# First stage of a two-block transformer kernel: the residual stream ahead of the gate tiles, one gate tile out of the chunk loop

## The chip, the cores and the metric

The kernel runs on one core of one Trainium2 chip, as one launch. The metric is the device time of that launch in microseconds, the median of several runs. PE is TensorE (its weight loads are shown apart as PEld), DVE VectorE, ACT ScalarE, POOL GpSimd, SP the engine whose queue issues nearly all transfers here.

## The reference, cut to what matters

Two blocks of two layers each work on 512 latent tokens and 256 context tokens of width 1024. The change touches only the very start, the first half of the first layer's mixer:

```python
mod  = silu(c)     @ ada_w[0] + ada_b[0]      # 6 vectors of 1024 for the latent tokens
modc = silu(c_ctx) @ ada_w[0] + ada_b[0]      # the same for the context tokens
sh1, sc1, ... = split(mod, 6)
a  = rmsnorm(h,  norm1_g[0]) * (1 + sc1)  + sh1     # modulate
ac = rmsnorm(hc, norm1_g[0]) * (1 + csc1) + csh1
# even_mixer
u, v, q, k, vv = split(a @ w_in, ...)         # u and v are 512 wide each
...
# chunk_mlp, the gating part of the mixer
u  = gelu(u)
vf = gelu(v);  vf = (vf - mean) * rsqrt(var + eps)   # by groups of 128 columns
mixed = einsum('gpq,bnqgc->bnpgc', w_s, vf) + b_s    # over 128 tokens
out = u * mixed
```

The matrices are drawn in float32. A product of the gate is computed as three products of rounded parts: high by high, high by low and low by high.

## The kernel before, in words

The 768 tokens lie along the free dimension and the 1024 features in 8 chunks of 128 partitions: `k.h` is [128, 8, 768]. The program is a row of stages, each a block with one instruction list for each engine. The first stage, `gating_mlp`, does the following.

**Stream.** `k.h` is loaded, ACT squares each chunk (`StreamSums.scalar`, L582), PE sums the squares over the partitions with a matrix of ones (L565). DVE forms the mean (L809), ACT the root (`norm.roots`, L732), DVE the reciprocal (L813) and its split in a high and a low part (L621, L623), and PE spreads it over all partitions (`norm.tensor`, L631 and L632) into PSUM banks 0 and 1.

**Modulation.** `FirstModulation` needs 16 tiles of 512 KB of `ada_w`, two for each chunk c (shift and scale). `mod.load(sp, c)` issues them (L2201), into places that are free this early: the buffers `mo`, `q`, `key` and `v` and the ring slots 2 to 4. `mod.multiply(pe, c)` makes 32 matmuls (L250), `mod.copy(act, c)` copies the two rows out of PSUM (L2224), `mod.turn(pe, c)` turns them into columns (L2231), and DVE's `mod.finish` adds the bias and makes the gain (L2238, L2241).

**Chunks.** For each chunk DVE scales the stream (`norm.scale`, L781), ACT adds the shift and rounds to the high part (`norm.high`, L748), and DVE makes the low part (`norm.low`, L767). DVE's order is finish(c), scale(c), low(c-1).

**Gate tiles.** The columns of `w_in` come as tiles of 128 columns, [128, 8 x 128], through the ring (`feed.issue`, L141). Each is split in a high part by ACT (`split.write_high`, L204) and a low part by POOL or DVE (`split.write_low`, L211). Entries 0, 1, 2 and 7 are the four tiles of u, entries 3 to 6 those of v. Entry 0 accumulates in PSUM banks 4 and 5, entry 1 in banks 6 and 7, entry 2 in banks 2 and 3, which the modulation uses until its last chunk. `tile_step(n, c)` multiplies chunk c of entry n (L2302, L2303, L2306), and waits for the high and the low part of that chunk. `tile_products` multiplies all chunks of an entry (L228).

**PE's order** is the loop over `step`: multiply(step), tile_step(0, step - 2), turn(step), tile_step(1, step - 4), with the spread behind multiply(0). Steps 8 to 11 do what is left of the two tiles. Then come entry 2 whole, the six token tiles of v, entry 7, and the mixing over tokens.

**SP's queue** is a list written by hand: small vectors, entries 0 and 1, the pick matrix (L262), the stream in four transfers of two chunks, the 16 modulation tiles, and after the third multiply the entries 2 to 7.

Of the kernel before, what the change touches and what calls it, by code (L numbers as in the profile page):

```python
# [16 lines left out]
ACT = mybir.ActivationFunctionType  # L17
AX = mybir.AxisListType

P = 128  # L20
D = 1024
KC = D // P
LAT, CTX = 512, 256
TOK = LAT + CTX
# [300 lines left out]
def spans(tokens):  # L325

    return [(0, LAT, 0), (LAT, TOK, 1)] if tokens == TOK else [(0, LAT, 0)]
# [6 lines left out]
def program(nc, io, out):  # L334
# [4 lines left out]
    with ExitStack() as ctx:  # L339
# [29 lines left out]
        with mixer(k, True, TOK, (4, TOK, 4, 512)):  # L369
            with ExitStack() as k.tmp:  # L370
                gating_mlp(k)
            project_in(k, "diff_in", DIFF_WORK, 5, TOK, rope=True)
# [156 lines left out]
def region(k, r, n=TOK):  # L529

    return k.psf[:, 1024 * r:1024 * r + n]
# [432 lines left out]
def tile_products(k, pe, i, j, dst, src, tokens, split=None, chunks=range(KC), first=True, last=True, between=None):  # L964

    slot = split.wait(pe, i, j) if split else k.feed.wait(pe, i, j)
    for a, b, _ in spans(tokens):
        if a and between:
            between()
        for n, c in enumerate(chunks):  # L970
            lo, hi = first and n == 0, last and n == len(chunks) - 1
            cols = slice(n * P, (n + 1) * P)
            if split:
                mm = split.products_of(pe, dst[:, a:b], (split.high[:, slot, cols], split.low[:, slot, cols]),
                                       (src[0][:, c, a:b], src[1][:, c, a:b]), lo, hi)
            else:
                mm = pe.matmul(dst[:, a:b], k.ring[:, slot, cols], src[:, c, a:b], start=lo, stop=hi)
    if split:
        mm.then_inc(split.products, 1)
    else:  # L980
        k.feed.done(mm, j)
# [1263 lines left out]
def gating_mlp(k):  # L2245

    nc, feed = k.nc, k.feed
    T, G = TOK // P, 4
    with Stage(k, "gating") as st:
        split = Split(k, st, 5, places=(0, 1, 4, 2, 3, 0, 1, 4))  # L2250
        mod = FirstModulation(k, st)
        norm = rms_stream(k, st, TOK, "mixer", 0, bank=3, r=0, squares=k.mo[:, 0:4, :])
        norm.by_pool, norm.shifts = (), k.mod[:, 0:KC, :]
        h_landed = [st.sem(f"h_landed{n}") for n in range(4)]
        ones_ready, loaded = st.sem("ones_ready"), st.sem("stream_loaded")
        sums = StreamSums(k, st, TOK, 3, loaded, 0, [norm.sq[:, c, :] for c in range(4)])
        u, v = k.q, k.v
# [9 lines left out]
        ENTRY = (0, 1, 2, 7)  # L2267
        U_REGION, MIX_REGION, V_BANK = (2, 3, 1, 3), (0, 1, 0, 1), (0, 1, 4, 5)

        @st.block.sync  # L2270
        def _(sp):
            sp.dma_start(k.small[:, :], k.io["small"]).then_inc(mod.small_landed, 16)
            for e in range(2):
                feed.issue(sp, 0, 0, only=e)
            mod.products.load(sp)
            for n in range(4):
                sp.dma_start(k.h[:, 2 * n:2 * n + 2, :], k.io["h0"][:, 2 * n:2 * n + 2, :]).then_inc(h_landed[n], 16)
            for c in range(KC):
                mod.load(sp, c)
            sp.wait_ge(mod.multiplied, 3)  # L2280
            for e in range(2, 8):
                feed.issue(sp, 0, 0, only=e)
            sp.dma_start(wst[:, :, :], k.io["sgu_wt"]).then_inc(landed, 16)
            sp.wait_ge(mod.turned, KC)
            sp.dma_start(rows, k.io["rows"][ROWCOL["sgu_b"]:NROWS].partition_broadcast(P)).then_inc(landed, 16)
            feed.issue(sp, 1, 0, ahead=True)
# [6 lines left out]
        @st.block.tensor  # L2293
        def _(pe):
            def tile_step(n, c):
                slot, cols, dst = split.place(ENTRY[n]), slice(c * P, (c + 1) * P), region(k, U_REGION[n])
                pe.wait_ge(norm.high_ready, c + 1)
                if c == 0:
                    split.wait(pe, 0, ENTRY[n])
                for a, b, _ in spans(TOK):  # L2300
                    high, values = split.high[:, slot, cols], k.hn[0][:, c, a:b]
                    pe.matmul(dst[:, a:b], high, values, start=c == 0, stop=False)  # L2302
                    pe.matmul(dst[:, a:b], split.low[:, slot, cols], values, start=False, stop=False)  # L2303
                norm.wait(pe, c)
                for a, b, _ in spans(TOK):
                    mm = pe.matmul(dst[:, a:b], split.high[:, slot, cols], k.hn[1][:, c, a:b], start=False, stop=c == KC - 1)  # L2306
                if c == KC - 1:
                    mm.then_inc(split.products, 1)

            def mix(g):  # L2310
                pe.wait_ge(normed, g + 1)
                if g == 1:
                    pe.wait_ge(u_ready, 3)
                if g >= 2:
                    pe.wait_ge(done, g - 1)
                for t in range(T):
                    mm = pe.matmul(region(k, MIX_REGION[g])[:, t * P:(t + 1) * P], v[:, t, g * P:(g + 1) * P], wst[:, g, :],
                                   start=True, stop=True)
                mm.then_inc(mixed, 1)

            def first_mixes():
                pe.wait_ge(landed, 32)
                mix(0)
                mix(1)

            split.start(pe)
            pe.wait_ge(ones_ready, 1)
            for c in range(KC):
                sums.tensor(pe, c)
            for step in range(KC + 4):  # L2330
                if step < KC:
                    mod.multiply(pe, step)
                if step == 0:
                    norm.tensor(pe)
                if 0 <= step - 2 < KC:
                    tile_step(0, step - 2)
                if step < KC:
                    mod.turn(pe, step)
                if 0 <= step - 4 < KC:
                    tile_step(1, step - 4)  # L2340
            tile_products(k, pe, 0, ENTRY[2], region(k, U_REGION[2]), k.hn, TOK, split)
            for e in range(3, 7):
                split.wait(pe, 0, e)
            for t in range(T):
                if t == 2:
                    pe.wait_ge(u_ready, 1)
                if t >= 4:
                    pe.wait_ge(v_ready, t - 3)
                wide_token_products(k, pe, k.ps[:, V_BANK[t % 4], :], k.hn, t, slice(0, 4), split).then_inc(v_done, 1)
            pe.sem_inc(split.products, 4)  # L2350
            pe.wait_ge(u_ready, 2)
            tile_products(k, pe, 0, ENTRY[3], region(k, U_REGION[3]), k.hn, TOK, split, between=first_mixes)
            mix(2)
            mix(3)

        @st.block.scalar
        def _(act):
            def gelu_u(g):
                split.wait_done(act, 0, ENTRY[g])
                act.activation(u[:, g, :], region(k, U_REGION[g]), ACT.Gelu).then_inc(u_ready, 1)  # L2360

            act.wait_ge(mod.small_landed, 16)
            mod.products.scalar(act)
            act.wait_ge(ones_ready, 1)
            norm.sums.build(act)
            for e in range(2):
                split.write_high(act, 0, e)
            act.sem_inc(loaded, KC)
            for c in range(KC):
                if c % 2 == 0:  # L2370
                    act.wait_ge(h_landed[c // 2], 16)
                sums.scalar(act, c)
            norm.roots(act)
            mod.copy(act, 0)
            for c in range(KC):
                if c + 1 < KC:
                    mod.copy(act, c + 1)
                else:
                    split.write_high(act, 0, 2)
                norm.high(act, (c,))  # L2380
            for e in range(3, 7):
                split.write_high(act, 0, e)
            for g in range(3):
                gelu_u(g)
            split.write_high(act, 0, 7)
            for t in range(T):
                act.wait_ge(v_done, t + 1)
                act.activation(v[:, t, :], k.ps[:, V_BANK[t % 4], :], ACT.Gelu).then_inc(v_ready, 1)
            act.wait_ge(var_ready, 1)
            act.activation(rstd[:, :, :], mv[:, :, :, 1], ACT.Sqrt, bias=k.eps[:, 0:1]).then_inc(root_ready, 1)  # L2390
            gelu_u(3)

        @st.block.vector
        def _(dve):
# [2 lines left out]
            dve.memset(k.eps[:, 1:2], GN_EPS).then_inc(ones_ready, 1)  # L2397
            mod.products.vector(dve)
            dve.wait_ge(mod.small_landed, 16)
            for n in range(4):  # L2400
                dve.wait_ge(h_landed[n], 16)
            dve.wait_ge(sums.summed, KC)
            norm.factor(dve)
            dve.wait_ge(norm.spread, 1)
# [1754 lines left out]
```

## Time and profile before

| | before |
|---|---|
| time, median of 3 runs | 3948.68 us (3947.75 to 3951.07) |
| the profiled execution | 3951.66 us |
| its span | 3949.7 us |
| PE busy | 3692.0 us, 93% of the span, 33646 matmuls |
| DVE, ACT, POOL busy | 58%, 38%, 45% of the span |
| the stretch before entry 2's products | 0 to 59.81 us |
| mean granted clock of PE | 0.952 |

The span is the time from the first to the last instruction; what lies around it is in the execution's own time. In a timeline a row begins with the start and the length in us, and a row with xN stands for N instructions in a row; the length is then that of the whole run. In brackets stands how long the engine was idle before, and what released it. SPq rows are issues of transfers, not the transfers themselves. Matmul lengths overlap: the distance of their starts is the rate.

### The profile page before, as it was taken

To read this page: it belongs to the slowest core of one execution; us is meant where nothing else is said; L and a number is where in the kernel's file an instruction comes from. 1 tells how busy PE (TensorE), PEld (TensorE's weight loads), DVE (VectorE), ACT (ScalarE), POOL (GpSimd) and SP (SyncE) were. 2 spreads that over 40 slices of the span, in tenths; PEclk is the share of its full clock that TensorE was granted. 3 is DMA by queue.
4 is the path that set the end of the run, shared out by engine and by line. 5 is a ranking of instruction groups with operands and counts; after the bars stand their busy time and mean duration, and the time that the engine had idled before them with its cause. 6 is when DMAs were issued, how large, how long until landed. Compare 5 with 4: busy or idle time off the path is not lost. (4 is left out here: it accounts for less than half of the span.)

```text
span 3949.7 us, 82111 instructions
## 1 busy us (share of the span) xinstructions
PE 3692.0 (93%) x33646; PEld 3232.8 (82%) x33646; DVE 2308.5 (58%) x4366; ACT 1507.1 (38%) x2831; POOL 1783.8 (45%) x1218
## 2 busy tenths in 40 slices
PE   8989899999998999989799999989999999989997
PEld 6867799998776888778698888769999878668996
DVE  4354566666553767675557775276666640737665
ACT  3244433333364444332234443253333242644443
POOL 0201555553343877532234432165555332737884
PEclk9999999999999999989779999989999999999998
DMA  5132233332201444332201100233333121012331
GB/s 189 60 121 96 91 118 107 108 116 82 71 6 61 154 160 158 127 111 106 79 19 32 29 21 25 81 107 102 113 107 109 68 71 58 24 56 73 105 99 64
DMA packets 159986, 343.83 MB, mean 87 GB/s; under 512 B 33535, under 2 KB 89343, under 8 KB 159359
## 3 DMA queue, kind: packets, MB, share of 16 engines
q1 hardware_dynamic: 139743, 266.23, 20.4%
q10 hardware_dynamic: 19872, 72.36, 5.3%
q8 instruction: 268, 4.39, 0.5%
q14 instruction: 103, 0.84, 0.1%
HBM read 323.74 MB, written 16.93 MB: 86 GB/s over the span
## 5 line engine op out<-in xcount | busy, mean ns | idle before, releaser
L1351 POOL TENSOR_TENSOR feed_low<-feed_sums,feed_high 128x512 fp32r<-128x512 f32 x320 | 502.9, 1592 | 467.5 <-ACT feed_high L1345 459.3
L1351 POOL TENSOR_TENSOR feed_low<-ring,feed_high 128x512 fp32r<-128x512 f32 x448 | 594.8, 1343 | 193.0 <-ACT feed_high L1345 96.2
L1345 ACT ACTIVATE feed_high<-ring 128x512 fp32r<-128x512 f32 x448 | 278.9, 626 | 433.4 <-PE ps L1596 244.1
L1580 PE MATMUL ps<-hn_high,feed_high 128*128 128x384 f32 (+1 forms) x1280 | 401.8, 314 | 0.0
L1581 PE MATMUL ps<-hn_low,feed_high 128*128 128x384 f32 (+1 forms) x1280 | 395.4, 309 | 0.0
L1582 PE MATMUL ps<-hn_high,feed_low 128*128 128x384 f32 (+1 forms) x1280 | 395.3, 309 | 0.0
L1594 PE MATMUL ps<-feed_hid,feed_high 128*128 128x384 f32 (+1 forms) x1056 | 379.7, 360 | 12.9 <-DVE h L1778 5.4
L1595 PE MATMUL ps<-feed_hid,feed_high 128*128 128x384 f32 (+1 forms) x1056 | 377.0, 357 | 0.0
L1596 PE MATMUL ps<-feed_hid,feed_low 128*128 128x384 f32 (+1 forms) x1056 | 376.6, 357 | 0.0
L1345 ACT ACTIVATE feed_high<-feed_sums 128x512 fp32r<-128x512 f32 x320 | 189.7, 626 | 486.9 <-DVE feed_sums L1370 315.6
L1580 PE MATMUL ps<-cross_high,feed_high 128*128 128x384 f32 (+1 forms) x960 | 297.9, 310 | 6.5 <-issue 5.7
L1581 PE MATMUL ps<-cross_low,feed_high 128*128 128x384 f32 (+1 forms) x960 | 297.6, 310 | 0.0
L1582 PE MATMUL ps<-cross_high,feed_low 128*128 128x384 f32 (+1 forms) x960 | 297.4, 310 | 0.0
L1580 PEld LDWEIGHTS ps<-hn_high,feed_high 128*128 128x128 f32 x1280 | 242.7, 190 | 52.8 <-issue 34.4
L1581 PEld LDWEIGHTS ps<-hn_low,feed_high 128*128 128x128 f32 x1280 | 242.9, 190 | 0.0
L1582 PEld LDWEIGHTS ps<-hn_high,feed_low 128*128 128x128 f32 x1280 | 242.8, 190 | 0.0
L1778 DVE SCALAR_TENSOR_TENSOR h<-ps,mod_even,h 128x384 f32<-128x384 f32 x528 | 219.8, 474 | 32.1 <-PE ps L1596 25.2
L3370 POOL TENSOR_TENSOR rwkv_ct<-h,rwkv_level_masks 128x384 f32<-128x384 f32 x108 | 127.9, 1207 | 231.1 <-DVE h L4000 185.5
L1594 PEld LDWEIGHTS ps<-feed_hid,feed_high 128*128 128x128 f32 x1056 | 199.0, 188 | 34.4 <-DVE h L1778 6.6
L1596 PEld LDWEIGHTS ps<-feed_hid,feed_low 128*128 128x128 f32 x1056 | 199.0, 188 | 16.2
L1595 PEld LDWEIGHTS ps<-feed_hid,feed_high 128*128 128x128 f32 x1056 | 199.1, 189 | 13.7
L1790 DVE TENSOR_TENSOR feed_hid<-feed_gate,feed_hid 128x768 fp32r<-128x768 f32 (+1 forms) x88 | 111.1, 1262 | 141.1 <-ACT feed_hid L1688 139.4
(645 smaller groups left out, 9500.7 us busy)
## 6 DMA issues: line engine op xcount, KB each, us to landing
feed_side_ring<-in_ada ACTq DMA_DIRECT2D x138, 512.0 KB, 4.3
ring<-in_ffn_g SPq DMA_DIRECT2D x88, 512.0 KB, 4.9
ring<-in_ffn_u SPq DMA_DIRECT2D x88, 512.0 KB, 3.6
ring<-in_ffn_d SPq DMA_DIRECT2D x88, 512.0 KB, 3.8
diff_side_ring<-in_ada SPq DMA_DIRECT2D x32, 512.0 KB, 4.2
ring<-in_od_in SPq DMA_DIRECT2D x24, 512.0 KB, 3.9
ring<-in_ev_in SPq DMA_DIRECT2D x23, 512.0 KB, 4.8
ring<-in_even_in SPq DMA_DIRECT2D x20, 512.0 KB, 4.4
```

Source lines behind the costliest of these rows:

```text
L1345: act.activation(self.high[:, e % self.SLOTS, :], self.source(name, n), ACT.Copy).then_inc(self.high_ready, 1)
L1351: pool.tensor_tensor(self.low[:, slot, :], self.source(name, n), self.high[:, slot, :].bitcast(F32), ALU.subtract).then_inc(self.low_ready, 1)
L1580: pe.matmul(dst, high, vh, start=c == 0, stop=False)
L1581: pe.matmul(dst, high, vl, start=False, stop=False)
L1582: mm = pe.matmul(dst, low, vh, start=False, stop=c == 3)
L1594: pe.matmul(dst, high, values[0], start=i == 0, stop=False)
L1595: pe.matmul(dst, high, values[1], start=False, stop=False)
L1596: mm = pe.matmul(dst, low, values[0], start=False, stop=i == 1)
L1778: ins = dve.scalar_tensor_tensor(out=hs, in0=src[:, lo - a:hi - a], scalar=k.mod[:, t + gate_at * KC, s:s + 1], in1=hs, op0=ALU.mult, op1= ...
L1790: dve.tensor_tensor(hidden(n, 1), gate(n), hidden(n, 0).bitcast(F32), ALU.subtract).then_inc(hid_low_ready, 1)
L3370: return pool.tensor_tensor(ct[:, d, gs, :], lt[d][:, gs, 0, :], levels[:, d, l, :].unsqueeze(1).to_broadcast([P, GR, RC]), ALU.mult)
```

## The change

The stream is fetched in eight transfers of one chunk, directly after the small vectors and the pick matrix. Entries 0 and 1 are issued behind the modulation tiles of chunk 0 and of chunk 1. ACT computes one root of a constant into a new tile `table` at its start, and its two `write_high` of entries 0 and 1 move behind mod.copy(0). On PE, turn(step) comes before the spread in step 0; the loop has 8 steps and works on entry 0 only; behind it come entry 0's last two chunks and entry 1 by `tile_products`.

```diff
-        h_landed = [st.sem(f"h_landed{n}") for n in range(4)]
+        h_landed = [st.sem(f"h_landed{c}") for c in range(KC)]
+        table = st.sb("table", [P, 1])
 ...
             sp.dma_start(k.small[:, :], k.io["small"]).then_inc(mod.small_landed, 16)
-            for e in range(2):
-                feed.issue(sp, 0, 0, only=e)
             mod.products.load(sp)
-            for n in range(4):
-                sp.dma_start(k.h[:, 2 * n:2 * n + 2, :], k.io["h0"][:, 2 * n:2 * n + 2, :]).then_inc(h_landed[n], 16)
+            for c in range(KC):
+                sp.dma_start(k.h[:, c, :], k.io["h0"][:, c, :]).then_inc(h_landed[c], 16)
             for c in range(KC):
                 mod.load(sp, c)
+                if c < 2:
+                    feed.issue(sp, 0, 0, only=c)
 ...
-            for step in range(KC + 4):
-                if step < KC:
-                    mod.multiply(pe, step)
+            for step in range(KC):
+                mod.multiply(pe, step)
+                if step >= 2:
+                    tile_step(0, step - 2)
+                mod.turn(pe, step)
                 if step == 0:
                     norm.tensor(pe)
-                if 0 <= step - 2 < KC:
-                    tile_step(0, step - 2)
-                if step < KC:
-                    mod.turn(pe, step)
-                if 0 <= step - 4 < KC:
-                    tile_step(1, step - 4)
+            for c in range(KC - 2, KC):
+                tile_step(0, c)
+            tile_products(k, pe, 0, ENTRY[1], region(k, U_REGION[1]), k.hn, TOK, split)
             tile_products(k, pe, 0, ENTRY[2], region(k, U_REGION[2]), k.hn, TOK, split)
 ...
             act.wait_ge(ones_ready, 1)
+            act.activation(table[:, :], k.eps[:, 0:1], ACT.Sqrt)
             norm.sums.build(act)
-            for e in range(2):
-                split.write_high(act, 0, e)
             act.sem_inc(loaded, KC)
             for c in range(KC):
-                if c % 2 == 0:
-                    act.wait_ge(h_landed[c // 2], 16)
+                act.wait_ge(h_landed[c], 16)
                 sums.scalar(act, c)
             norm.roots(act)
             mod.copy(act, 0)
+            for e in range(2):
+                split.write_high(act, 0, e)
 ...
             dve.wait_ge(mod.small_landed, 16)
-            for n in range(4):
-                dve.wait_ge(h_landed[n], 16)
+            for c in range(KC):
+                dve.wait_ge(h_landed[c], 16)
```

## Rows read from the trace of the kernel before

**Rows 1.** Timeline, first 6 us: the stream's four issues; ACT's pick tile.
```profile
2.83 2.56 SPq L2277 DMA_DIRECT2D h<-in_h  x4
...
3.95 1.26 ACT L610 ACTIVATE gating_pick<-ones 32x128 fp32r<-32x128 f32 x4
```

**Rows 2.** One line's issues and landings: gate tiles, stream, three modulation tiles (second of chunk 1, two of chunk 2).
```profile
L141 SPq DMA_DIRECT2D ring<-in_even_in x2: 420/426/432, 1.2 to 1.6; - x2
...
DMA to landing us min/median/max: 3.8/4.5/5.2
...
DMA to landing us min/median/max: 6.4/8.2/10.1
...
L2201 SPq DMA_DIRECT2D ring<-in_ada x3: 442/443/461, 7.2 to 8.2; - x3
...
DMA to landing us min/median/max: 12.7/13.4/15.3
```

**Rows 3.** Timeline, 14 to 21 us: last squares to the spread.
```profile
14.79 1.58 ACT L582 ACTIVATE mo<-h 128x768 f32<-128x768 f32 x2 [0.31 <-DMA h<-in_h]
...
16.38 1.28 ACT L732 ACT_TABLE_LOAD   x1
...
17.12 0.36 DVE L809 TENSOR_SCALAR gating_factor<-ps 128x192 f32<-128x192 f32 x1 [6.07 <-PE ps L565]
...
17.46 1.08 PE L250 MATMUL ps<-mo,gating_mod_vec 128*32 128x128 f32 x32 [0.51 <-DMA mo<-in_ada]
17.68 0.36 ACT L732 ACTIVATE gating_factor<-gating_factor 128x192 f32<-128x192 f32 x1
...
20.25 0.53 PE L631 MATMUL ps<-gating_factor_high,gating_pick 128*128 128x192 f32 x1 [1.71 <-DVE gating_factor_low L623]
```

**Rows 4.** Timeline, 22 to 31 us: turn(0), product 1, product 2, turn(2).
```profile
22.34 0.97 PEld L2231 LDWEIGHTS ps<-gating_mod_pick,gating_ada_rows 128*128 128x128 f32 x4
...
23.33 1.08 PE L250 MATMUL ps<-mo,gating_mod_vec 128*32 128x128 f32 x16
...
26.71 1.93 PE L250 MATMUL ps<-ring,gating_mod_vec 128*32 128x128 f32 x32
...
30.59 0.50 PE L2231 MATMUL ps<-gating_mod_pick,gating_ada_rows 128*128 128x2 f32 x4
```

**Rows 5.** Timeline, 34 to 39 us: one period of the chunk loop.
```profile
34.59 0.50 PE L2231 MATMUL ps<-gating_mod_pick,gating_ada_rows 128*128 128x2 f32 x4
...
36.93 1.14 DVE L767 SCALAR_TENSOR_TENSOR hn_low<-mo,mod_even,hn_high 128x512 fp32r<-128x512 f32 x2
...
38.12 0.61 PE L2306 MATMUL ps<-hn_low,gating_high 128*128 128x512 f32 x2 [1.13 <-DVE hn_low L767]
```

**Rows 6.** Timeline, 50 to 69 us: end of the loop, entry 2, first products of v.
```profile
50.56 0.50 PE L2231 MATMUL ps<-gating_mod_pick,gating_ada_rows 128*128 128x2 f32 x4
...
54.10 0.62 PE L2306 MATMUL ps<-hn_low,gating_high 128*128 128x512 f32 x2 [1.20 <-DVE hn_low L767]
...
59.81 0.39 PE L228 MATMUL ps<-hn_high,gating_high 128*128 128x512 f32 x1
...
68.15 0.40 PE L228 MATMUL ps<-gating_high,hn_high 128*128 128x512 f32 x1
```

**Rows 7.** Busy time by stretch: us, PE, PEld, DVE, ACT, POOL; clock, DMA share, GB/s.
```profile
18.00:20.00 2.00, 0.54 (x20) 0.27 (x12) 1.78 (x3) 0.42 (x2) 0.00 (x0) 1.00 1.02 410
...
30.00:32.00 2.00, 2.00 (x40) 1.73 (x38) 0.69 (x4) 0.10 (x1) 0.00 (x0) 0.88 1.03 412
...
36.00:40.00 4.00, 2.87 (x20) 2.33 (x16) 2.78 (x8) 1.51 (x3) 0.00 (x0) 1.00 1.03 410
40.00:44.00 4.00, 4.00 (x50) 3.15 (x48) 2.77 (x8) 1.39 (x3) 0.00 (x0) 1.00 0.25 97
```

**Rows 8.** Timeline, 6 to 11 us: POOL's two low parts, one DVE add.
```profile
6.37 4.66 POOL L211 TENSOR_TENSOR gating_low<-ring,gating_high 128x1024 fp32r<-128x1024 f32 x2 [5.95 <-ACT gating_high L204]
...
8.88 2.17 DVE L273 TENSOR_TENSOR gating_mod_pick<-gating_mod_pick 128x2 f32<-128x2 f32 x1
```

## The prediction

> **What bounds the kernel now.** All that the change touches lies in the first stage, so I read the timeline of its first 70 us, then where single transfers landed, then the granted clock by stretch. That stretch has three parts with three limits.
>
> First, up to 20.25 us, the transfers and a chain behind them. The queue issues two gate tiles (1.2 and 1.6 us) before the residual stream (from 2.83). They land at 1.2 + 3.8 = 5.0 and 1.6 + 5.2 = 6.8; the stream's first pair of chunks is there only at 2.8 + 6.4 = 9.2, its last at 14.79 [rows 1 to 3]. Two squares end at 16.37; then the sums, the mean (17.12), the root (17.68), reciprocal and split on DVE, and at 20.25 the spread starts on PE [rows 3]. There is a table load at 16.38, but it ends at 17.66 and the mean that the root waits for at 17.48. The first modulation product waits for its two tiles until 17.46; the second has its tiles at 7.23 + 12.7 = 19.9, the third its second tile at 8.18 + 15.3 = 23.5 [rows 2, 3].
>
> Second, the loop over chunks. The `turn` matmuls of chunk 3 start at 34.59, those of chunk 7 at 50.56: four periods of 3.99 us [rows 5, 6]. The reader should see what closes one period: turn, DVE's two adds and the gain, the scaling, then the low part of the chunk before (36.93, ends 38.07), and only then PE's last products of that chunk (38.12, after 1.13 idle), and the next turn [rows 5]. The products of gate tile 1 lie at 38.91 to 40.16, in the hole of PE that this circle leaves open.
>
> Third, from 54.10 (last low of chunk 6) PE has no gap: the last chunks of tiles 0 and 1, then tile 2 from 59.81 to 68.15 [rows 6], then the token products. After 54.10 any work taken from or given to PE moves everything behind it one for one.
>
> **The change, part by part.** Times are against the profiled execution (3951.66 us, span 3949.7, so 1.96 outside the span); it stands 2.98 above the median of the runs.
>
> 1. *The two gate tiles leave the place ahead of the stream.* That is 1 MiB. Two tiles of this size take 17.46 - 14.79 = 2.67 us, two others 19.9 - 17.4 = 2.5 [rows 2, 3]; at the start one took 6.8 - 5.0 = 1.8, so 3.6 for two [rows 2]. The last chunk then lands between 11.2 and 12.3; I take 12.3, and ACT, whose building of the pick tile ends at 5.2 now and at 6.7 with 1.5 of table and root ahead of it, then needs 8 x 0.79 and is no earlier than 13.1 by either [rows 1, 3]. ACT's squares are 0.79 each, and only one is left after the last landing instead of two: the last ends at 13.1 to 13.2 instead of 16.37. Sums 0.75, mean 0.36, root 0.36, reciprocal and split to 16.9. Gain: 3.3 us at the point where the spread could start.
>
> 2. *Eight transfers instead of four.* Four more issues, 0.65 each at most [rows 1], 2.6 us of SP's queue. SP has the room: eight issues at 0.65 are 5.2 us for a stream that needs some 7.5 to land. The half-sized chunks give the 0.79 of item 1. The price is nothing as long as the transfers stay queued; the third modulation chunk has the same bytes ahead of it as before, so its landing stays 23.5 [rows 2].
>
> 3. *The table loaded early.* The load takes 1.28 and the root started 0.20 after its mean was ready [rows 3]: worth 0.1 to 0.2, already in item 1. ACT does it between 3.4 and 5, before the first chunk lands.
> The Trainium skill ("ScalarE: Activation LUTs", What ACT_TABLE_LOAD costs) puts a switch at some 2.66 us with its drain. The row has 1.28 and the root 0.02 behind it, so the drain is not seen; by the page's figure the early load would give up to 1.4 us more.
>
> 4. *turn(0) ahead of the spread.* Product 0 now waits for its tiles at 14.8, ends at 15.9, is copied by 16.35, and turn(0) runs 16.4 to 16.9 at the full clock (0.50 + 0.12 from the later rows) or to 17.4 at the half one (before, it held PE from 22.34 to 23.32 [rows 4, 5]). It lies almost wholly in the wait for the root. It delays the spread by 0 to 0.5 and takes 1 us from behind it.
>
> 5. *ACT copies tiles 0 and 1 (1.06 each) after copy(0), and the second lies behind modulation chunk 1 in the queue.* It lands about where chunk 1 does now, 19.9. So ACT is held until 21.0; queued behind are copy(1), the first high part and so turn(1). With the half clock, product 1 ends at 21.6 (before: from 23.33, at 1.93 for 32 matmuls [rows 4]) and the wait is covered; with the full clock it ends near 19.8 and copy(1) is held 1.2 us.
>
> The clock decides between the two. It was granted full (2.4 GHz) until 20 us and half (1.2 GHz) after 1.7 us of idle PE; it came back at about 31 [rows 3, 7]. Half clock again: product 2 starts at 23.5, held 0.4 by its tiles, against 26.71, gain 3.2; the step after it is unchanged. Full clock: product 2 at 23.5 to 24.6, tile 0's chunk to 25.5, low part at 25.2, turn(2) ends at 26.4 instead of 31.09, gain 4.7. PE's holes in the new order are shorter (1.1 and 0.5 us), but the rows cannot tell; I take the middle, **4.0 us**, bounds 3.2 and 4.7.
>
> 6. *Tile 1 leaves the loop.* Steps 4 to 7 lose four chunks of tile 1. The circle of 3.99 does not contain them: step 3, without any of them, has PE idle 1.13 and the same period [rows 5]. Gain in the loop: 0. What the loop gained is kept, all behind it shifts by the 4.0.
>
> 7. *Tile 1 behind the loop.* Call the end of turn(7) t, now 51.07. Before, tile 2 starts at 59.81 = t + 8.74. After: last products of chunk 6 at t + 3.03 (its low part sets that, as now), to t + 3.38; chunk 7 of tile 0, 0.70 for the high ones, its low part at t + 4.25, done at t + 4.62; then a whole tile, which tile 2 shows to be 68.15 - 59.81 = 8.34 [rows 6]; tile 2 starts at t + 12.96. Cost **4.2 us**. That is simply four chunks at 1.04 which had been free.
>
> Sum: -4.0 + 4.2 = +0.2, from -0.5 to +1.0. The later copies of ring tiles that wait for tile 1's products come earlier relative to tile 2's end than needed (8.34 us of cover against 1.06 + 1.23). Span 3949.9, execution 3951.9, median **3948.9 us**: no change. What a measurement here can tell is about 0.2%, 7.9 us, far more than either term.
>
> **The rivals.**
>
> *A. The loop's gain survives.* If PE, full in steps 4 to 7 (4.00 of 4.00 [rows 7]), were itself the limit there, taking 1.04 from each of four would pay for the tile behind: 4.2 more, 3944.7. Against it: steps 3 and 4 to 7 have one period. With the largest gain of the front (4.7 + 0.5 for an earlier stream) it would be 3943.5. Chance 5%, still within 0.2%.
>
> *B. The clock falls in the emptied loop (the slower side).* PE works 2.87 of 4 us in such a step, and rows 7 show that this kept the full clock over steps 3 and 4; but five such steps follow each other now. If it falls, each step costs 4.38 - 3.99 = 0.4 more (the half-clock step from 26.71 to 31.09 [rows 4]), 2.0 in all; the clock came back some 4 us after PE was full (26.7 to 31), which in tile 1 costs 2. Sum +4, with +0.2: 3953. It decides the sign for the measurement only if the half clock lasts through the whole tile, 8.3 us more: +10.5, 3959. Chances 12% and 3%.
>
> *C. A lock between POOL and DVE.* POOL's low part of tile 0 (about 2.3 us, 4.66 for two) ran until 11.03, and a 2-column DVE add that began at 8.88 ended at 11.05; it takes 2.17 instead of 0.15 [rows 8]. Now this POOL work starts at 17.5, behind the split of the root (to 16.9); should the root be 0.7 late, its two SBUF reads are caught, up to +2.3: 3951. Chance 8%.
> The Trainium skill ("SBUF — State Buffer", SBUF: two separate sides) says that whichever of the two starts first holds the shared port pair for its whole instruction, and counts DVE ops with two SBUF inputs. The row agrees; by that rule the risk is all or nothing, as priced.
>
> *D. The smaller transfers run slower.* Before, 512 KB took 1.8 us at the very start and 1.3 later [rows 2, 3]. No row shows chunks of 384 KB; if all 3 MiB of the stream went at the early rate, that is 6 x 0.5 = 3.0 us, and gate tile 1, for which ACT now waits, comes as much later. Half of it as the likely size: 3950.4, at most 3951.9. Chance 10%.
>
> *E. The change does nothing:* the stream isn't the limit. Rows 3 exclude it, the waits for it are there.
>
> **Numbers.** My forecast (3948 to 3950 by its terms) 62%, A 5%, B 15%, C 8%, D 10%. The range adds what single runs differ by (3.3 us between the fastest and the slowest) and B's smaller case: 3944 to 3954. Faster by over 0.2% needs more than all bounds together: 3%. Slower by over 0.2%: the 3% of B and 1% for what I don't see. Within: 93%.
>
> **What the profile of the changed kernel would show.** Last square's end near 13.1; root with no table load before it; spread near 17 instead of 20.25; ACT's copy of gate tile 1 ending near 21; turn(2) ending between 26.4 and 27.9; periods of 4.0 with PE idle about 1.1 in each; after turn(7) (46.4 to 47.9) 3.0 us to chunk 6's last products, a run of 8.3 us for tile 1, tile 2 starting at 59.3 to 60.8 against 59.81. The forecast is wrong if the periods shrink (A), if the granted clock shows half after 31 us (B), if a DVE op of 2 us stands near 17 to 23 (C), or if tile 1's run costs less than 8.3.

## The result: slower by 0.24%, which the forecast had at 4 in 100

Over 21 runs the changed kernel takes 3957.09 us in the median (3950.74 to 3979.81), the kernel before, run beside it on the same chip, 3949.41 (3941.54 to 3956.31). The ratio is 1.0024 with a 95% interval of 1.0014 to 1.0033, some 5.5 to 13 us slower. Forecast were 3948.9 and no change.

The profiled execution of the changed kernel took 3954.94 us, its span is 3952.4. First the timeline of its first 25 us (start, length, engine, line, operation). L2276 is now the line of the stream's transfers, L2365 that of the early root.

```profile
1.89 4.22 SPq L2276 DMA_DIRECT2D h<-in_h  x8
3.33 1.28 ACT L2365 ACT_TABLE_LOAD   x1
...
10.17 3.76 ACT L582 ACTIVATE mo<-h 128x768 f32<-128x768 f32 x4 [0.16 <-DMA h<-in_h]
...
15.02 0.36 DVE L809 TENSOR_SCALAR gating_factor<-ps 128x192 f32<-128x192 f32 x1 [11.01 <-PE ps L565]
...
15.76 1.93 PE L250 MATMUL ps<-mo,gating_mod_vec 128*32 128x128 f32 x32 [0.91 <-DMA mo<-in_ada]
...
17.57 0.36 DVE L623 TENSOR_TENSOR gating_factor_low<-gating_factor,gating_factor_high 128x192 fp32r<-128x192 f32 x1
...
18.28 0.99 PE L2231 MATMUL ps<-gating_mod_pick,gating_ada_rows 128*128 128x2 f32 x4 [0.58 <-ACT gating_ada_rows L2224]
...
19.12 0.51 PE L631 MATMUL ps<-gating_factor_high,gating_pick 128*128 128x192 f32 x1
...
21.48 1.08 PE L250 MATMUL ps<-mo,gating_mod_vec 128*32 128x128 f32 x16
```

Against [rows 3]: the last square ends at 13.9 instead of 16.37, the mean is formed 2.1 us earlier, the table load is out of the way. But product 0 takes 1.93 us for the same 32 matmuls that took 1.08, turn(0) follows it at 18.28, and the spread, whose inputs are ready at 17.93, starts at 19.12. Of the 2.4 us gained at the last square 1.1 are left at the spread.

Then the end of the loop and what stands behind it, in the same view, to compare with [rows 6]. L2307 is now the line of the products with the low part.

```profile
48.34 0.50 PE L2231 MATMUL ps<-gating_mod_pick,gating_ada_rows 128*128 128x2 f32 x4
...
51.88 1.01 PE L2307 MATMUL ps<-hn_low,gating_high 128*128 128x512 f32 x2 [2.23 <-DVE hn_low L767]
...
54.60 0.63 PE L228 MATMUL ps<-hn_high,gating_high 128*128 128x512 f32 x1
...
64.16 0.40 PE L228 MATMUL ps<-hn_high,gating_high 128*128 128x512 f32 x1
```

turn(7) starts 2.2 us earlier, entry 2 (the second L228 run here, at 64.16) 4.35 us later than before. PE is idle for 2.23 us ahead of chunk 6's last products, where it was idle for 1.20. Entry 1 takes 54.60 to 64.16, 9.56 us for what entry 2 does in 8.34. Busy time by stretch says why; the columns are those of [rows 7], the third from the right is the granted clock.

```profile
32.00:36.00 4.00, 2.87 (x43) 2.32 (x43) 2.77 (x7) 1.50 (x3) 0.00 (x0) 1.00 1.02 406
36.00:40.00 4.00, 4.00 (x43) 3.37 (x43) 2.77 (x7) 1.39 (x3) 0.00 (x0) 0.59 1.03 410
40.00:44.00 4.00, 2.87 (x44) 2.32 (x43) 2.77 (x7) 1.51 (x3) 0.00 (x0) 0.99 0.44 170
...
48.00:52.00 4.00, 1.77 (x11) 1.43 (x11) 2.82 (x8) 2.07 (x4) 0.00 (x0) 0.79 0.00 0
52.00:56.00 4.00, 4.00 (x12) 3.32 (x13) 4.00 (x5) 2.88 (x3) 0.00 (x0) 0.50 0.18 55
56.00:60.00 4.00, 4.00 (x17) 3.22 (x16) 1.64 (x2) 0.00 (x0) 0.00 (x0) 0.85 0.77 276
```

Behind three steps in which PE was idle for 1.13 to 1.18 us (it is busy 2.87 of 4 us in the window before 36 us) the clock falls to half (1.2 GHz) from about 36.7 to 40, and again from about 50.4 to 57, right where PE must do the work that was moved there. In the trace of the kernel before it was full from 30.5 us to the end of the stage.

### The profile page after: what moved, and what is told of

It is laid out like the page before. It is cut to its first block and busy times, and to the rows that moved or that the text cites. A ratio compares the mean times of both kernels' runs of the same rounds, so it can differ in the third digit from the quotient of the medians.

```text
span 3952.4 us, 82119 instructions
## 1 busy us (share of the span) xinstructions
PE 3693.2 (93%) x33646; PEld 3233.8 (82%) x33646; DVE 2306.0 (58%) x4366; ACT 1507.0 (38%) x2832; POOL 1783.7 (45%) x1218
```

## The experiments

Times of single runs spread by several us and a few reach 3975 to 3984, so each kernel is read in two ways: by the ratio to the kernel before on the same chip, and by marks in its trace. The marks are the starts of turn(7), of entry 2 and of the next stage's first transfer (L1904). The matmul durations in a trace tell the clock that PE had.

| kernel | turn(7) | entry 2 | next stage | median | ratio, 95% interval |
|---|---|---|---|---|---|
| before | 50.56 | 59.81 | 118.3 | 3949.41 | 1 |
| before_again | 51.54 | 60.81 | 119.3 | 3955.34 | 1.0005 (0.9988 to 1.0023) |
| changed | 48.34 | 64.16 | 122.7 | 3957.09 | 1.0024 (1.0014 to 1.0033) |
| after_again | 50.48 | 65.67 | 124.2 | 3958.57 | 1.0019 (1.0001 to 1.0038) |
| after_third | 49.91 | 65.20 | 123.7 | 3957.53 | 1.0024 (1.0008 to 1.0041) |
| front_only | 48.77 | 58.04 | 116.5 | 3950.84 | 0.9998 (0.9980 to 1.0015) |
| front_only_again | 49.35 | 58.62 | 117.1 | 3953.55 | 1.0018 (0.9998 to 1.0038) |
| loop_only | 49.78 | 64.54 | 123.0 | 3957.24 | 1.0013 (0.9996 to 1.0030) |
| after_filled | 49.24 | 63.54 | 122.0 | 3959.20 | 1.0017 (0.9995 to 1.0038) |
| after_warm | 48.44 | 62.74 | 121.2 | 3956.62 | 1.0017 (1.0001 to 1.0033) |
| after_e1_dve | 49.39 | 64.66 | 122.8 | 3957.74 | 1.0011 (0.9995 to 1.0027) |
| after_turn_behind | 48.81 | 63.59 | 122.1 | 3959.53 | 1.0019 (1.0007 to 1.0032) |
| front_e1_dve | 50.33 | 59.60 | 117.7 | 3952.07 | 0.9998 (0.9983 to 1.0014) |
| front_four | 49.38 | 58.65 | 117.1 | 3952.16 | 0.9998 (0.9983 to 1.0013) |
| front_best | 50.24 | 59.50 | 117.7 | 3950.62 | 1.0011 (0.9992 to 1.0031) |
| front_light | 49.42 | 58.69 | 116.8 | 3949.08 | 0.9981 (0.9964 to 0.9999) |
| front_light_again | 49.88 | 59.15 | 117.3 | 3951.44 | 1.0003 (0.9984 to 1.0021) |

The reader should see two groups. With entry 1 in the loop the next stage starts at 116.5 to 119.3, with it behind the loop at 121.2 to 124.2, whatever else is changed.

**The changed kernel again (after_again).** No edit.

> The changed kernel once more, for a second trace of it. Theory 1 (the clock falls in the emptied loop): the granted clock shows half in at least one stretch between 30 and 60 us, entry 2's products start about 3.5 to 5.5 us later than before (59.81), and the rest of the shift is noise of later stages. Theory 2 (something in a later stage pays): entry 2 starts within 1 us of 59.8 in this trace, and the span is longer by what a later stage adds. Time by either: 3955 to 3959.

Entry 2 starts at 65.67, 5.9 us late, a little over the forecast of 5.5. Here PE was at half clock until about 35 (product 2 took 1.93 for 32 matmuls), full in the loop, and half again from 55.3 to 58.7. Theory 1 holds: the first stage pays.

**The front alone (front_only).** The changed kernel with the old loop:

```diff
-            for step in range(KC):
+            for step in range(KC + 4):
...
-            for c in range(KC - 2, KC):
-                tile_step(0, c)
-            tile_products(k, pe, 0, ENTRY[1], region(k, U_REGION[1]), k.hn, TOK, split)
+                if 0 <= step - 4 < KC:
+                    tile_step(1, step - 4)
```

> The front of the change alone: stream in eight parts first, gate tiles behind, table and turn ahead, ACT's two copies moved, but entry 1 stays in the chunk loop. Theory 1: the loop is full and keeps the clock from step 4 on, the front's gain of about 2.4 us stays: 3945 to 3948. Theory 2 (the new front itself costs, by the clock of its first 30 us or by later stages): 3951 or more.

The marks are 1.8 us ahead of the kernel before all through the stage. In time it can't be told from it: 3950.84 us, beside 3952.38 for the kernel before on the same chip, and not the 3945 to 3948 expected.

**The loop alone (loop_only).** The kernel before with entry 1 behind the loop.

```diff
-            for step in range(KC + 4):
+            for step in range(KC):
...
-                if 0 <= step - 4 < KC:
-                    tile_step(1, step - 4)
+            for c in range(KC - 2, KC):
+                tile_step(0, c)
+            tile_products(k, pe, 0, ENTRY[1], region(k, U_REGION[1]), k.hn, TOK, split)
```

> The loop edit alone on the kernel before: entry 1 multiplied whole behind the loop, everything at the front as before. Theory 1: 4.2 us for the four chunks that had been free, and 2 to 4 us for a clock that falls in the loop and comes back within entry 1: 3955 to 3958. If only the four chunks cost: 3953.6. Theory 2: no change, 3949.

From turn(7) to entry 2 it takes 14.76 us instead of 9.25: 5.5 more, of which 4.2 were forecast. Its clock, in the view by stretch:

```profile
44.00:48.00 4.00, 2.87 (x40) 2.41 (x39) 2.78 (x9) 1.13 (x3) 0.00 (x0) 0.77 0.00 0
...
52.00:56.00 4.00, 2.68 (x8) 2.30 (x9) 3.87 (x7) 3.02 (x4) 0.00 (x0) 0.62 0.00 0
```

Here too the clock falls once entry 1 is out of the loop, with the old front: from 46.1 to 49.5 us and from 53.0 to 56.4. In time the run is 4.9 us over the kernel before, as forecast, but its interval still includes 1.

**PE's hole filled (after_filled).** Ahead of `norm.wait` in `tile_step`:

```diff
+                for _ in range(9 if c == 6 else 4):
+                    pe.matmul(region(k, 3)[:, 0:512], split.high[:, slot, cols], k.hn[0][:, c, 0:512], start=True, stop=True)
```

> The changed kernel with matmuls that fill PE's hole in each chunk (four of 512 columns into the idle banks of entry 1, nine at chunk 6; their result is not used). If the idle hole is what drops the clock, the granted clock stays full from 30 us on, entry 2 starts near 61.6 instead of 64.2, and the time is 2 to 3 us under the changed kernel's, 3952 to 3955. If the clock falls for another reason, it stays near 3957.

```profile
48.00:52.00 4.00, 3.81 (x21) 2.96 (x19) 2.77 (x8) 2.07 (x4) 0.00 (x0) 1.00 0.00 0
52.00:56.00 4.00, 3.83 (x19) 2.93 (x18) 3.87 (x6) 3.26 (x5) 0.00 (x0) 1.00 0.00 0
```

With PE busy 3.8 of 4 the clock is full from 28 us on, and entry 1 takes 8.34. From turn(7) to entry 2 it takes 14.30, of which 0.9 are the fillings of chunk 7: about 13.4, the 13.5 of the forecast. So the excess of the changed kernel over the forecast in this stretch (15.82 - 13.47 = 2.35) is the half clock. Entry 2 starts 0.6 us sooner than in the changed kernel, 2 us less than I expected, and the median is 3959.20 instead of 3952 to 3955: in time the filling gained nothing that can be seen.

Where the clock was half between 34 and 60 us separates the traces, but not quite as theory 1 says:

| traces | half clock, us |
|---|---|
| entry 1 behind the loop, no filling | changed 36.7 to 40.1 and 50.4 to 57.2; after_again 55.3 to 58.7; after_third 50.7 to 57.6; after_e1_dve 50.2 to 57.1; loop_only 46.1 to 49.5 and 53.0 to 56.4; after_turn_behind 45.2 to 48.6 and 52.0 to 55.4 |
| entry 1 behind the loop, filled | after_filled and after_warm: none |
| entry 1 in the loop | none in six traces; front_e1_dve 37.8 to 41.2; front_best 37.6 to 41.0; front_four 36.7 to 40.1 |

In all six unfilled traces the clock is half for part of the work behind turn(7); in none of the other eleven is it half after 41.2. But the loop with entry 1 in it isn't safe either: in three of nine traces the clock falls in the step behind turn(4), right behind the last of the idle stretches that entry 1 does not yet fill (1.12 to 1.14 us; in each of the three it is the only one over 0.6 us since 30 us), and that step then takes 5.3 us instead of 3.99. Nor is the longest idle stretch, ahead of chunk 6's last products, what it takes. In after_third the clock falls while PE is busy, before that stretch begins:

```profile
46.00:50.00 4.00, 2.86 (x45) 2.32 (x43) 2.77 (x7) 2.01 (x4) 0.00 (x0) 1.00 0.00 0
50.00:51.00 1.00, 1.00 (x8) 0.86 (x7) 0.45 (x3) 0.44 (x1) 0.00 (x0) 0.87 0.00 0
```

```profile
53.45 1.01 PE L2307 MATMUL ps<-hn_low,gating_high 128*128 128x512 f32 x2 [1.95 <-DVE hn_low L767]
```

**The kernel before again (before_again).** No edit.

> The kernel before once more, for a second trace of it. If the first stage alone pays, its marks repeat within 1 us (turn of chunk 7 at 50.6, entry 2 at 59.8, next stage at 118.3), and later stages differ by up to 3 us between traces. If its first trace was a lucky one in the clock, entry 2 comes 1 to 2 us later here. Time: the same as before.

The marks repeat within 1 us. In this trace the clock was half until 31.8 by the durations of its matmuls (product 0 took 1.93), where the first trace had it full from 13.4 to 20.2. Its own ratio, 1.0005 with 0.0018 either way, shows what such a comparison can tell.

**Entry 1's split out of the way (after_e1_dve).**

```diff
-            for e in (0, 1, 7):
+            for e in (0, 7):
                 split.write_low(pool, 0, e)
...
-            for e in range(2):
-                split.write_high(act, 0, e)
+            split.write_high(act, 0, 0)
...
+                if c == 0:
+                    split.write_high(act, 0, 1)
...
+                if c == 1:
+                    split.write_low(dve, 0, 1)
```

> The changed kernel with entry 1's split out of the way: ACT copies its high part behind the first high part of the stream, and DVE, not POOL, makes its low part, behind low(0). If the lock between POOL and DVE and ACT's wait for entry 1's tile cost the front 1 to 2 us, no gain computation (L2241) takes over 0.3 us after 21 us, and turn(2) starts at 27.5 to 28.5 in half clock, against 29.5. If they are hidden: no difference, or 1 us worse by DVE's added 1.23 us. Time 3954 to 3957 in the first case, 3957 to 3959 in the second.

It answers to a row of after_again, and the same pair is in the timelines of after_third and of both traces of front_only (in the first trace of the changed kernel that gain takes 0.23, and the next one 0.50):

```profile
22.23 2.35 POOL L211 TENSOR_TENSOR gating_low<-ring,gating_high 128x1024 fp32r<-128x1024 f32 x1 [0.37 <-ACT gating_high L204]
22.36 2.24 DVE L2241 TENSOR_SCALAR gating_norm_gains<-mod_even,small 128x2 f32<-128x2 f32 x1
...
24.69 1.14 DVE L781 SCALAR_TENSOR_TENSOR mo<-h,gating_norm_gains,ps 128x512 f32<-128x512 f32 x2
```

A gain of two columns that takes 0.23 us elsewhere takes 2.24 and ends as POOL's instruction ends. With the split moved it is 0.23 again. turn(2) starts at 29.08 against 29.54 and 29.41 in the two repeats: a gain of 0.3 to 0.5, not the 1 to 2 expected. DVE's own 1.22 us are not the reason: they end at 29.31, and DVE waits for turn(2) until 29.94. The reason is that the 2 us of the lock lay for the most part in a wait: without it DVE is idle for 1.50 us ahead of its next chunk, until turn(1) is done. The lock is real and cost half a us.

**The changed kernel with PE warm from the start (after_warm).** As after_filled, and matmuls of `ones` by `ones` in PE's waits: 20 before the first sum, three behind each sum, product 0, turn(0) and product 1.

> The changed kernel with matmuls on constants in all waits of PE from 2 us on (20 first, three behind each sum, product 0, turn 0 and product 1) and those of the filled loop; their results are not used. If PE's clock is what the new order loses at the front, it is full through spread and products: spread at 17.5, turn(2) near 27, turn(7) near 47, entry 2 near 61, time 3950 to 3953. If the clock is not the cause, turn(2) stays at 28 to 29.5.

The clock is full from 5 us to the stage's end, but three of these matmuls take 0.87 us, more than PE had between two sums, and the mean comes at 17.77 instead of 15.02. Even so turn(7) is at 48.44 and the next stage at 121.2, the earliest of this group. From mean to turn(7) it takes 30.7 us; 33.3 in the changed kernel, 35.1 in after_again, and 33.4 and 33.6 in the two traces of the kernel before. Not all of that is the clock: with a mean 2.75 us later, products 0 to 2 find their tiles landed, where the changed kernel waits 0.91 us for those of product 0. And in after_filled, without any filling there, the clock was full from 10.9 to 17.7 us and the spread started at 17.55, but turn(2) only at 29.26. Entry 2 is at 62.74 and the median 3956.62, where some 61 and 3950 to 3953 were expected.

**The same split moved in the front alone (front_e1_dve).** front_only with the edit above.

> The front alone with only the split of entry 1 moved, no filling. If the 2.24 us gain computation under POOL's instruction was on the path, it is 0.23 here, and turn(2) starts at 28.0 to 28.5 against 28.79. If DVE's added 1.23 us takes that back, turn(2) or turn(3) is where it was. Time 3948 to 3952.

The gain of two columns takes 0.23 us for every chunk here too, but turn(2) starts at 28.74, against 28.79 and 29.04 in the two traces of front_only (13.8 us behind the mean, against 14.4 and 14.5), turn(7) at 50.33 and the next stage at 117.7. The clock falls to half from 37.8 to 41.2 us, which neither trace of front_only shows there, so the marks behind it are later. In time nothing is seen, with a ratio of 0.9998.

**The front with split and filling (front_best).** front_only, the split moved as above, the constant matmuls of after_warm, and four fillings each at chunks 0 and 1.

> The front of the change with entry 1 back in the loop, its split moved as in the run before the last, and the constant matmuls in PE's waits until chunk 1. Theory 1 (four chunks in the hole are free, the clock and the lock ate the front's gain): turn(2) at 26 to 27.5, turn(7) at 46 to 47.5, entry 2 at 55.3 to 57, time 3944 to 3947, faster than before. Rival: the fillings delay the chain they stand in, or entry 1's low part on DVE does, and it gains no more than the 1.8 us of the front alone, 3948 to 3951.

The mean comes at 18.45 for the same reason, the next stage at 117.7. The rival of this run held: the fillings stand in the chain. The clock falls here too, from 37.6 to 41.0, and takes another 1.3 us.

**Lighter filling (front_light, front_light_again).** front_best with 18 constant matmuls first, one behind each sum, two more behind the last, one behind products 0 and 1, and none behind turn(0).

> The front of the change with entry 1 in the loop and its split moved, and a lighter filling: 18 constant matmuls before the first sum, one behind each sum, two behind the last, one behind products 0 and 1, none before the spread. In the heavier filling three of them took 0.94 us behind each sum, and the sums ended 3 us late; here sum and filling are 0.76 us, under the 0.94 us between chunks. If that was all that held it: clock full from 7 us, spread at 17 to 17.6, turn(2) at 25.5 to 27, turn(7) 46 to 47, entry 2 at 55 to 56.5, next stage at 113.5 to 115, time 3944 to 3948. If the clock falls again between the sums, turn(2) at 28 and next stage at 116.5 as with the front alone.

> The front with entry 1 in the loop, its split moved and the light filling, a second time: was its ratio of 0.9981 real? By its first trace only 1.5 to 2.5 us came in the first stage (next stage at 116.8), so I expect the same stage start within 1 us and a ratio of 0.999 to 1.000. If the filling gave something more, the ratio is 0.998 again.

The spread starts at 17.76 in both, 2.5 us before [rows 3], and turn(2) only at 29.44 and 29.91. Timeline of the first:

```profile
19.49 2.35 POOL L211 TENSOR_TENSOR gating_low<-ring,gating_high 128x1024 fp32r<-128x1024 f32 x1 [19.07 <-ACT gating_high L204]
19.57 2.28 DVE L2241 TENSOR_SCALAR gating_norm_gains<-mod_even,small 128x2 f32<-128x2 f32 x1
20.94 0.80 PE L250 MATMUL ps<-mo,gating_mod_vec 128*32 128x128 f32 x16 [1.85 <-DMA ring<-in_ada]
```

The gain of the spread is taken back by the tiles of product 1 (PE idle 1.85), then by those of product 2 (0.78), by entry 0's low part on POOL, and by a clock that falls at 21.3 in these waits. The first ratio lay under 1 with its whole interval; the second, 1.0003, does not repeat it. No faster version is shown.

**Four transfers (front_four).** front_only with the stream in four transfers of two chunks.

> The front alone, but the stream in four transfers of two chunks. If the eight parts bring what the squares say (one square of 0.79 instead of two behind the last landing), the last square ends 0.6 to 0.9 us later than in the front alone (13.6 to 13.9 there), the mean as much later. If smaller transfers run slower, the last landing is earlier here and it cancels. Time as the front alone within the noise, 3949 to 3953.

The mean starts at 14.61, against 14.36 and 14.51 in the two traces of the front alone. The eight parts bring 0.1 to 0.25 us, not 0.8, and even that is less than the traces with eight parts and no fillings at the front differ among themselves (their last squares end between 13.6 and 14.6, here at 13.86). The landings say why; first this run, then front_only:

```profile
L2276 SPq DMA_DIRECT2D h<-in_h x4: 431/518/707, 1.9 to 3.5; - x4
...
DMA to landing us min/median/max: 4.7/6.6/8.8
```

```profile
L2276 SPq DMA_DIRECT2D h<-in_h x8: 432/436/739, 1.9 to 5.7; - x8
...
DMA to landing us min/median/max: 4.1/5.6/7.0
```

In four transfers the stream has landed at 3.5 + 8.8 = 12.3, in eight at 5.7 + 7.0 = 12.7, and at 13.1, 13.4 and 13.1 in the three traces of the changed kernel. So the second case of the expectation came true: eight parts land later, and that eats the square that they save. The modulation tiles behind them move along. Product 0 waits for its tiles until 14.95 here, 15.43 and 15.59 in the front alone; product 2 until this row, and until 24.65 to 24.88 in the runs with eight parts whose timeline shows that wait:

```profile
23.79 1.93 PE L250 MATMUL ps<-ring,gating_mod_vec 128*32 128x128 f32 x32 [1.84 <-DMA ring<-in_ada]
```

turn(2) starts at 27.75, the earliest of all 17 traces, and turn(4) at 36.08, 0.7 us before the better trace of front_only. Then this trace loses 1.3 us to a clock that falls from 36.7 to 40.1. Part of the lead can be a full clock around product 0, so four transfers are not shown to be better, but they are no worse. Why the eight land later stays open.

**turn(0) behind the spread (after_turn_behind).**

```diff
-                mod.turn(pe, step)
                 if step == 0:
                     norm.tensor(pe)
+                mod.turn(pe, step)
```

> The changed kernel with turn(0) behind the spread again. If turn(0) ahead delays the spread as the trace says (split ready at 17.93, spread at 19.12), the spread starts at 17.9 to 18.3 here, but product 1 starts at 21.2 to 21.5 as with it ahead, since the same matmuls lie in between: no difference in turn(1). If the order matters, turn(1) moves by 0.5 or more. Time as the changed kernel, 3955 to 3959.

From the mean to the spread it takes 2.97 us (15.68 to 18.65) where the changed kernel takes 4.10, and to product 1 6.04 where it takes 6.46. At half clock, by this one trace, turn(0) ahead of the spread costs 0.4 us.

**The last repeats (after_third, front_only_again).** No edits.

> The changed kernel a third time. The first stage explains +4.4 and +5.9 us in two traces, the timed runs +7.7 and +6.2. If nothing else pays, the next stage starts at 122 to 124.5 here too (before: 118.3 and 119.3), the stretch from there to the end differs from the kernel before by its noise only (3831.4 and 3832.2 there), and the timed difference over all runs comes down towards 5. If a later stage pays 2 to 3 us, that stretch is 3834 or more in all three traces.

> The front of the change alone a second time. By its first trace it gains 1.8 us up to entry 2, by its 12 runs 1.5 in the median with an interval of 0.998 to 1.0015. If the front's gain is real and nothing later takes it back: next stage at 116 to 117.5, ratio 0.999 to 1.000. If it was one lucky clock: next stage at 118 to 119.

From the next stage's start to the end of the span the three traces of the changed kernel take 3829.7, 3833.2 and 3822.7 us, the two of the kernel before 3831.4 and 3832.2. No later stage is seen to pay, though with traces of one kernel 10 us apart a cost of 1 or 2 us would not be seen. The front's gain in the marks, 1.2 to 2.2 us against the kernel before, is there again; its ratio is not told from 1.

Single comparisons are too coarse for these few microseconds, but the runs fall in two groups as the marks do. In the seven later experiments with entry 1 behind the loop the 81 timed runs have a median of 3958.4 us, in the seven with the new front and entry 1 in the loop the 82 runs have 3951.3. The difference of 7.1 us lies between 5.1 and 8.2 when the runs are drawn again at random; the next stage starts 5.5 us later in the mean of the first group.

## Why the prediction was wrong, step by step

What was right: item 6 holds (periods of 3.99 with PE idle 1.13; nothing gained in the loop), so does item 3 (the load vanishes, worth 0.2), and rival A is excluded. Item 7's 4.2 us was right for a full clock, as after_filled shows.

What failed is the balance of -4.0 and +4.2, on both sides: in the front by landings and by the clock, behind the loop by the clock.

- **The front's gain, forecast 4.0 with bounds of 3.2 and 4.7, is 1.5 us.** turn(7) started at 50.56 and 51.54 before, at 48.34, 50.48 and 49.91 after: means 51.05 and 49.58. The first step that failed is item 2, which put the price of eight transfers at nothing, and rival D, which thought of slower small transfers, had 10%. In the changed kernel the stream has landed at 13.1, not 12.3, so the last square ended at 13.9, not 13.1; product 0's tiles came at 15.76, not 14.8; product 2 started at 24.55, not 23.5; and gate tile 1, which item 5 had at 19.9, lets ACT's copy start at 21.88. With four transfers (front_four) the stream has landed at 12.3 and product 0's tiles at 14.95, as forecast, and product 2 starts at 23.79. The sums, at half clock, took 1.1 us to the mean instead of 0.75. Then item 5's lower bound assumed that half clock would start at the spread, as in the one trace I had. In all three traces of the changed kernel it was half from the first sum (product 0 in 1.93 or 1.94), so turn(0) of item 4 was not hidden but held the spread for 1.2 us, where I had allowed 0.5. Rival C's lock struck not the split of the root but the gain (L2241), and cost some 0.3 to 0.5. How the 2.5 us divide among these is not shown, for they overlap.
- **The cost behind the loop, forecast 4.2, is 5.9 to 6.6 us** (turn(7) to entry 2: 15.82, 15.19 and 15.29 instead of 9.25). The 1.7 to 2.4 above the forecast are rival B: the clock falls where the loop was emptied. I gave it 15%. It came in all six unfilled traces with entry 1 behind the loop, and was gone in the two where the holes were filled. The step that failed is item 7, which priced the moved tile and what stands before it at full clock: I had seen steps 3 and 4 keep the clock with PE idle for 1.13 us in each, and took that as good for the row of five. It was not even good for one: in front_e1_dve, front_best and front_four the clock falls right behind such a stretch. That the trace that I had kept it was luck in part. Whether the row of short holes or the long one ahead of chunk 6's last products counts for more is not separated, for the fillings closed both; in after_third and after_e1_dve the fall comes before the long one.
- Together the next stage starts at 123.5 instead of 118.8 (means of three and of two traces): 4.7 us later. In time that is a little under the first comparison, 5.5 to 13 us. The medians of the three comparisons, each beside the kernel before on the same chip, are 7.7, 6.2 and 6.1 us apart; over all runs, 45 of the changed kernel and 166 of the kernel before, they are 3957.8 and 3952.2, 5.6 apart. What the remaining 1 to 3 us are stays open, and so does whether they are anything.

The range, to 3954, was too narrow for a second reason. It took the spread of three runs of before; 21 runs spread over 15 us, and the stage's marks by 1 us between two traces of one kernel.

## What to carry to other kernels

Work that lies in another engine's hole is free twice: it costs no time, and it keeps TensorE's clock up for what comes behind. Before it is moved out, look at the row of idle stretches that it leaves and price what stands behind them at half clock; a single trace in which such a row kept the clock is no proof. And where a kernel starts cold, one trace's clock of the first 30 us is no bound; take the durations at half clock for the whole start as the lower case. A gain at the front must be followed through each wait behind it: here the next tiles' landing, a shared port and the clock each took a part. And a transfer cut in smaller pieces needs a price of its own: ask when the last piece lands, and what is queued behind it.

## What the runs showed of the hardware that was not expected

- **The granted clock of the first stretch isn't to be trusted.** In the changed kernel the view by stretch has 1.00 from 10 to 22 us, and in before_again all through the stage, while 32 matmuls of product 0 took 1.93 us in both, as at half clock; they take 1.08 at full. The durations of known matmuls tell the clock there.
- **A tiny DVE instruction with one SBUF tensor input is held by POOL.** L2241 on two columns took 2.24 and 2.28 us under a POOL instruction of 2.35, 0.23 without. Of such an op I had not thought; the Trainium skill ("SBUF — State Buffer", SBUF: two separate sides) has it, since it counts DVE ops in a 2-port mode as well as those with two SBUF inputs. The trace agrees with the first-come lock: POOL began at 22.23, L2241 at 22.36. That L2241 ran in a 2-port mode no run shows. Two L781, which read one input from PSUM, lay beside a POOL instruction for their last 0.5 us in the changed kernel, and neither side was longer for it (1.14 and 2.36).
- **A run near 3975 us had its clock down in far later stages.** The trace of loop_only was of such a run (3975.11), the only one traced. Around 2350 us, in the recurrent mixer, it has half clock throughout; the kernel before, in the same stretch of its trace, has not:

```profile
2347.00:2384.00 37.00, 35.03 (x666) 32.85 (x666) 19.83 (x38) 13.57 (x30) 11.44 (x8) 0.50 0.01 3
```

```profile
2347.00:2384.00 37.00, 34.19 (x974) 32.01 (x974) 28.76 (x60) 18.79 (x48) 14.91 (x11) 0.86 0.02 4
```

In the same 37 us it gets through 666 matmuls instead of 974. Both kernels have runs as long as this; that those have the same cause was not looked at, nor why it happens.
